# A two-block diffusion and sparse-attention kernel: column-halved opening modulation and a 112-candidate expert search

## The reference, cut to what matters

```python
m = (jax.nn.silu(c) @ w_mod[l] + b_mod[l]).reshape(B, N_MOD, D_MODEL)
mc = (jax.nn.silu(c_ctx) @ w_mod[l] + b_mod[l]).reshape(1, N_MOD, D_MODEL)
x = ffn_sublayer(x, m, 0, norm_g[l, 0], ffn_w_in[l, 0], ffn_w_out[l, 0])
# mod_norm(x, m, i, g) = rms_norm(x, g) * (1 + m[:, 3 * i + 1, None]) + m[:, 3 * i, None]
```

```python
v, i = lax.top_k(s, PEER_TOPK)
cand = (v[..., 0, :, None] + v[..., 1, None, :]).reshape(B, TB, PEER_HEADS, PEER_TOPK * PEER_TOPK)
tv, tj = lax.top_k(cand, PEER_TOPK)
w = jax.nn.softmax(tv, axis=-1)
a = jax.nn.gelu(jnp.einsum('btd,btpkd->btpk', hblk, u).astype(jnp.float32))
```

## Time and profile before

| | |
|---|---|
| median of three runs | 2854.39 us (2853.64 to 2857.55) |
| profiled execution, its own time | 2854.86 us |
| its span, first to last instruction | 2853.1 us |
| PE matmul busy | 2765.5 us (97%), 15702 records |
| DVE busy | 2095.5 us (73%) |
| ACT busy | 1211.4 us (42%) |
| POOL busy | 528.0 us (19%) |
| mean granted TensorE clock | 0.993 of full speed |

### The profile page before, as it was taken

The page is one execution under the profiler, slowest core; times in us unless marked ns, Lnnn a source line. Parts: engine busy times, 40 slices in busy tenths (PEclk is TensorE's granted clock), DMA queues, the critical chain, the costliest instruction groups (busy, mean ns, idle before and its releaser), DMA issues.

```text
span 2853.1 us, 40332 instructions
## 1 busy us (share of the span) xinstructions
PE 2765.5 (97%) x15702; PEld 2343.0 (82%) x15702; DVE 2095.5 (73%) x3770; ACT 1211.4 (42%) x2208; POOL 528.0 (19%) x447
## 2 busy tenths in 40 slices
PE   7999999989999999999988999998989999999998
PEld 4888887758888878888886999878989888888887
DVE  1989997477989897565766766755897677777776
ACT  2323234364222243222445545554556444444444
POOL 1111111500111111010040000344889100000000
PEclk9999999999999999999999999999999999999999
DMA  6455443223545445354441566423644555555564
GB/s 244 159 200 187 179 159 119 96 81 107 184 178 188 179 175 185 126 184 137 159 142 54 189 226 205 130 88 129 194 139 118 173 193 189 190 194 189 192 193 130
DMA packets 123262, 462.51 MB, mean 162 GB/s; under 512 B 13504, under 2 KB 26688, under 8 KB 109888
## 3 DMA queue, kind: packets, MB, share of 16 engines
q1 hardware_dynamic: 109248, 359.27, 38.1%
q0 software_dynamic: 13824, 100.67, 9.1%
HBM read 452.93 MB, written 6.95 MB: 161 GB/s over the span
## 4 chain that ended last, share of the span: by engine, by line
PE 85%; DVE 11%; issue 2%; ACT 1%; POOL 1%; DMA 0%; POOLq 0%; DVEq 0%; SPq 0%; ACTq 0%
PE bank L283 26%; PE bank L284 25%; PE bank L285 25%; DVE weight_lo L182 2%; PE bank L2309 2%; DVE extension_ffn L806 1%; PE bank L689 1%; PE bank L495 1%; DVE nmax L1280 1%; DVE arena L531 1%; PE bank L381 1%; PE bank L826 1%; PE bank L827 1%; ACT weight_hi L175 1%; DVE arena L2468 1%
## 5 line engine op out<-in xcount | busy, mean ns | idle before, releaser
L175 ACT ACTIVATE weight_hi<-weight_ring 128x512 fp32r<-128x512 f32 x1272 | 798.4, 630 | 1190.0 <-PE bank L285 1189.3
L182 DVE TENSOR_TENSOR weight_lo<-weight_ring,weight_hi 128x512 fp32r<-128x512 f32 x1110 | 839.2, 760 | 431.8 <-ACT weight_hi L175 429.9
L283 PE MATMUL bank<-operand_hi,weight_hi 128*128 128x256 f32 (+1 forms) x3168 | 1048.7, 331 | 26.3 <-DVE operand_lo L548 13.0
L284 PE MATMUL bank<-operand_lo,weight_hi 128*128 128x256 f32 (+1 forms) x3168 | 1034.6, 327 | 0.0
L285 PE MATMUL bank<-operand_hi,weight_lo 128*128 128x256 f32 (+1 forms) x3168 | 1034.1, 326 | 0.0
L283 PEld LDWEIGHTS bank<-operand_hi,weight_hi 128*128 128x128 f32 x3168 | 603.8, 191 | 96.9 <-issue 25.5
L284 PEld LDWEIGHTS bank<-operand_lo,weight_hi 128*128 128x128 f32 x3168 | 604.2, 191 | 53.7 <-issue 1.2
L285 PEld LDWEIGHTS bank<-operand_hi,weight_lo 128*128 128x128 f32 x3168 | 603.7, 191 | 50.6
L806 DVE SCALAR_TENSOR_TENSOR extension_ffn<-extension_ffn,silu_c 128x512 f32<-128x512 f32 x532 | 388.5, 779 | 1.7
L235 POOL TENSOR_TENSOR weight_lo<-weight_ring,weight_hi 128x512 fp32r<-128x512 f32 x162 | 214.6, 1334 | 431.2 <-ACT weight_hi L175 429.3
L283 PE MATMUL bank<-hidden_hi_ffn,weight_hi 128*128 128x512 f32 (+1 forms) x704 | 256.6, 364 | 4.0 <-DVE arena L1058 4.0
(11 more groups left out here) (259 smaller groups left out, 2616.5 us busy)
## 6 DMA issues: line engine op xcount, KB each, us to landing
weight_ring<-in_ffn SPq DMA_DIRECT2D x272, 512.0 KB, 3.5
weight_ring<-in_experts SPq DMA_DIRECT2D x256, 512.0 KB, 3.5
extension_ffn<-in_w_mods POOLq DMA_DIRECT2D x96, 1024.0 KB, 7.5
weight_ring<-in_w_mix SPq DMA_DIRECT2D x56, 512.0 KB, 3.5
weight_ring<-in_w_second SPq DMA_DIRECT2D x52, 512.0 KB, 3.6
spill<-early_retrieve SPq DMA_DIRECT2D x45, 128.0 KB, 3.8
arena<-spill SPq DMA_DIRECT2D x45, 128.0 KB, 3.4
extension_mixer<-in_rel_bias SPq DMA_DIRECT2D x2, 1536.0 KB, 6.8
```

Source lines behind the costliest of these rows:

```text
L175: nc.scalar.activation(self.hi[:, g % 2, h], self.ring[:, g % NS, h], ACT.Copy).then_inc(self.rounded, 1)
L182: self.nc.vector.tensor_tensor(self.lo[:, g % 2, h], self.ring[:, g % NS, h], self.hi[:, g % 2, h].bitcast(F32), ALU.subtract).then_inc(se ...
L283: nc.tensor.matmul(out, a_hi, b_hi, start=start and n == 0, stop=False)
L284: nc.tensor.matmul(out, a_hi, b_lo, start=False, stop=False)
```

## The change

In the opening, PE no longer sums eight pieces of squares: DVE adds them up (`gather`), and PE sums one piece, after modulation unit 4; the spread comes after unit 5. Each modulation unit goes in four pairs of matmuls, the first of a pair into partitions 0 and 1, the second into partitions 64 and 65 of a bank; four banks are used in turn, ACT copies both rows pairs, and the turn is now a matmul over 66 rows with a matrix `both` that adds the two halves. The turn comes two units behind. x is multiplied by the inverse root on DVE (`whiten`) before the gains are known; gain and shift are then applied by ACT in one instruction, and a second scaled copy (`again`), one token group by ACT and one by DVE, feeds the subtraction. The first weight unit is rounded and subtracted before the gains, and the second half of the second unit inside the operand loop. SP issues two weight units when modulation unit 6 is there and two when unit 7 is.

In retrieval, only the sums that can be among the 16 best are formed: left ranks 0 to 3 with all 16 right ranks and left ranks 4 to 15 with right ranks 0 to 3, 112 per head, in two instructions for all heads at once. `decode` gets three instructions to turn a position of 112 back into one of 256, and its integer positions and the index table lie in PSUM bank 7 instead of SBUF. The exponential of the first 128 tokens moves from behind down unit 18 to behind unit 16.

```diff
...
+class FirstNorm(Norm):
...
+    def whiten(self, dve):
+        dve.wait_ge(self.rstd_there.sem, self.rstd_there.at(1))
+        for kt in range(KT):
+            self.chip.nc.vector.tensor_tensor(self.h[:, kt, :], self.x[:, kt, :], self.rstd(0, T2), ALU.mult)\
+                .then_inc(self.scaled.sem, len(self.groups))
+    def round(self, act):
+        nc, n = self.chip.nc, len(self.groups)
+        act.wait_ge(self.gains_there.sem, self.gains_there.at(1))
+        for kt in range(KT):
+            if kt >= 4:
+                act.wait_ge(self.split_in.sem, self.split_in.at(kt - 3))
+            lo, hi = self.groups[1]
+            nc.scalar.activation(self.again[:, kt % 4, lo:hi], self.h[:, kt, lo:hi], ACT.Copy, scale=self.gain(kt, 1))
+            if kt == 2:
+                self.units.round(act, 0, 1, [1])
+            for g, (lo, hi) in enumerate(self.groups):
+                nc.scalar.activation(self.hi[:, kt, lo:hi], self.h[:, kt, lo:hi], ACT.Identity, bias=self.shift(kt, g),
+                                     scale=self.gain(kt, g)).then_inc(self.h_ready.sem, 1)
+    def again_scaled(self, dve, kt):
+        lo, hi = self.groups[0]
+        self.chip.nc.vector.tensor_scalar(self.again[:, kt % 4, lo:hi], self.h[:, kt, lo:hi], self.gain(kt, 0), None, ALU.mult)\
+            .then_inc(self.scaled_again.sem, 1)
+    def operands(self, dve):
+        self.again_scaled(dve, 0)
+        for kt in range(KT):
+            if kt + 1 < KT:
+                if kt >= 3:
+                    dve.wait_ge(self.split_in.sem, self.split_in.at(kt - 2))
+                self.again_scaled(dve, kt + 1)
+            dve.wait_ge(self.scaled_again.sem, self.scaled_again.at(kt + 1))
+            for g, (lo, hi) in enumerate(self.groups):
+                dve.wait_ge(self.h_ready.sem, self.h_ready.at(n * kt + g + 1))
+                last = nc.vector.scalar_tensor_tensor(self.lo[:, kt, lo:hi], self.again[:, kt % 4, lo:hi], self.shift(kt, g),
+                                                      self.hi[:, kt, lo:hi].bitcast(F32), ALU.add, ALU.subtract)
+            last.then_inc(self.split_in.sem, 1)
+            if kt == 1:
+                self.units.subtract(dve, 0, 1, [1])
+        dve.wait_ge(self.split_in.sem, self.split_in.at(KT))
...
-        sp.wait_ge(chip.mod_first[0].sem, 32)
-        self.stream.load(sp, 0, NS)
+        sp.wait_ge(chip.mod_first[2].sem, 32)
+        self.stream.load(sp, 0, 2)
+        sp.wait_ge(chip.mod_first[3].sem, 32)
+        self.stream.load(sp, 2, NS)
...
     def tensor(self, pe):
         chip, nc = self.chip, self.chip.nc
         def turn(l):
-            pe.wait_ge(self.copied.sem, self.copied.at(l + 1))
+            pe.wait_ge(self.copied.sem, self.copied.at(2 * l + 2))
             for b in range(2):
...
+                last = nc.tensor.matmul(chip.bank[2][:, 4 * l + 2 * b:4 * l + 2 * b + 2],
+                                        self.sums[0:66, l % 2, b * P:(b + 1) * P], chip.both[0:66, :], start=True, stop=True)
             last.then_inc(self.turned.sem, 1)
-        pe.wait_ge(chip.constants.sem, 1)
-        self.norm.sums(pe)
+        pe.wait_ge(chip.constants.sem, 2)
         pe.wait_ge(self.silued.sem, self.silued.at(1))
         for l in range(self.n):
             pe.wait_ge(chip.mod_first[l % self.slots].sem, 16 * (l // self.slots + 1))
+            if l >= 4:
+                pe.wait_ge(self.copied.sem, self.copied.at(2 * (l - 4) + 2))
+            for kt in range(0, KT, 2):
+                for j in range(2):
+                    last = nc.tensor.matmul(self.bank(l)[64 * j:64 * j + 2, 0:256], chip.silu_c[:, kt + j, :],
+                                            self.w[l % self.slots][:, (kt + j) * 256:(kt + j + 1) * 256],
+                                            start=(kt == 0), stop=(kt == KT - 2))
+            last.then_inc(self.first_summed.sem, 1)
             if l >= 2:
-                pe.wait_ge(self.copied.sem, self.copied.at(l - 1))
...
-            if l:
-                turn(l - 1)
-            if l == 1:
+                turn(l - 2)
+            if l == 4:
+                self.norm.sums(pe)
+            if l == 5:
                 self.norm.spread(pe)
+        turn(self.n - 2)
         turn(self.n - 1)
     def scalar(self, act):
         chip, nc = self.chip, self.chip.nc
+        def copy(l):
+            act.wait_ge(self.first_summed.sem, self.first_summed.at(l + 1))
+            if l >= 2:
+                act.wait_ge(self.turned.sem, self.turned.at(l - 1))
+            for j in range(2):
+                q = slice(64 * j, 64 * j + 2)
+                nc.scalar.activation(self.sums[q, l % 2, :], self.bank(l)[q, 0:256], ACT.Copy).then_inc(self.copied.sem, 1)
...
+        act.wait_ge(chip.constants.sem, 2)
         for kt in range(KT):
             self.norm.square(act, kt)
-        self.norm.root(act)
         for l in range(self.n):
...
-        for j in range(2):
-            self.units.round(act, 0, j)
+            if l == self.n - 1:
+                self.units.round(act, 0, 0)
+            copy(l)
+            if l == 3:
+                self.norm.root(act)
+        self.units.round(act, 0, 1, [0])
     def vector(self, dve):
         chip, nc = self.chip, self.chip.nc
+        def finish():
+            dve.wait_ge(self.turned.sem, self.turned.at(self.n))
...
         dve.wait_ge(self.loaded_x.sem, self.loaded_x.at(16))
+        for kt in range(1, KT):
+            self.norm.gather(dve, kt)
         self.norm.invert(dve)
...
-        finish_mod(chip, dve, 0, 0, 2)
-        for j in range(2):
-            self.units.subtract(dve, 0, j)
+        self.norm.whiten(dve)
+        self.units.subtract(dve, 0, 0)
+        finish()
+        self.units.subtract(dve, 0, 1, [0])
...
+CAND_ROWS = [(0, 0, 4, TOPK), (4 * TOPK, 4, TOPK, 4)]
+CANDS = 4 * TOPK + 4 * (TOPK - 4)
...
-TURN_AT, EXP_AT = [(ALONE - 1, 1), (ALONE + 14, 0)], [(ALONE - 2, 1), (ALONE + 13, 0)]
+TURN_AT, EXP_AT = [(ALONE - 1, 1), (ALONE + 14, 0)], [(ALONE - 4, 1), (ALONE + 13, 0)]
...
-        ixf = chip.part(E_IF, 2, 16, TOPK)
+        ixf = chip.bank[7][:, P:P + 16 * TOPK].rearrange("p (n k) -> p n k", k=TOPK)
...
-        jj, jf = chip.part(E_J, 2, SLOTS).bitcast(U32), chip.part(E_JF, 2, SLOTS)
+        jj, jf = chip.bank[7][:, P + 16 * TOPK:P + 16 * TOPK + SLOTS].bitcast(U32), chip.part(E_JF, SLOTS)
...
-        cand = chip.part(E_CAND, 2, PH, TOPK * TOPK)
+        cand = chip.part(E_CAND, 2, PH, CANDS)
...
             if first == 0:
-                step(nc.vector.tensor_copy(ixf[:, tt, :, :], ix[:, tt, :, :]))
+                if tt == 0:
+                    dve.wait_ge(self.table.sem, self.table.at(18))
+                step(nc.vector.tensor_copy(ixf, ix[:, tt, :, :]))
             vp = v[:, tt, :, :].rearrange("p (h two) k -> p h two k", two=2)
-            for h in range(first, last_h):
+            n = last_h - first
+            for at, a0, a1, nb in CAND_ROWS:
+                shape = [P, n, a1 - a0, nb]
                 last = nc.vector.tensor_tensor(
...
+                    cand[:, tt, first:last_h, at:at + (a1 - a0) * nb].rearrange("p h (a b) -> p h a b", b=nb),
+                    vp[:, first:last_h, 0, a0:a1].unsqueeze(3).to_broadcast(shape),
+                    vp[:, first:last_h, 1, 0:nb].unsqueeze(2).to_broadcast(shape), ALU.add)
...
+            step(nc.vector.tensor_scalar(jj, tj[:, tt, :], 4 * TOPK, 4 * TOPK, ALU.max, ALU.subtract))
+            step(nc.vector.tensor_scalar(jj, jj, 2, None, ALU.logical_shift_right))
+            step(nc.vector.scalar_tensor_tensor(tj[:, tt, :], jj, TOPK - 4, tj[:, tt, :], ALU.mult, ALU.add))
             for half in range(2):
-                step(nc.vector.tensor_scalar(jj[:, half, :], tj[:, tt, :], 4 if half == 0 else 15, None,
+                step(nc.vector.tensor_scalar(jj, tj[:, tt, :], 4 if half == 0 else 15, None,
                                              ALU.logical_shift_right if half == 0 else ALU.bitwise_and))
...
+                step(nc.vector.tensor_copy(jf, jj))
                 more(tt)
                 step(nc.vector.tensor_tensor(eq, iota16.unsqueeze(1).to_broadcast([P, SLOTS, TOPK]),
...
+                                             jf.unsqueeze(2).to_broadcast([P, SLOTS, TOPK]), ALU.is_equal))
                 more(tt)
                 e4 = eq.rearrange("p (h k) i -> p h k i", h=PH)
-                sub = ixf[:, tt, :, :].rearrange("p (h two) k -> p h two k", two=2)[:, :, half, :]
+                sub = ixf.rearrange("p (h two) k -> p h two k", two=2)[:, :, half, :]
...```

PE in the opening, from the program's first instruction to the first weight unit. Before (`arena` holds the squares, `extension_ffn` a modulation unit or the copied rows):

```order
L495 MATMUL bank<-ones,arena 128x2 x32
L689 MATMUL bank<-extension_ffn,silu_c 2x256 x16
L677 MATMUL bank<-ident,extension_ffn 128x2 x2
L517 MATMUL bank<-ident,rstd 128x128 x4
L689 MATMUL bank<-extension_ffn,silu_c 2x256 x8
```

71 lines of the change are left out of this document (40 added, 31 removed).

## The result

The changed kernel takes 2814.87 us (median of 4 runs, 2813.83 to 2818.67), the kernel before 2854.32 us in the same session (4 runs). The ratio is 0.9863, with a 95% interval of 0.9851 to 0.9875. The forecast was 2815, between 2808 and 2827. The profiled execution took 2814.13 us, 40.7 less than before, and its span is 2812.3. Of the runs of the kernel before that serve as comparison on other chips further down, one of 6799.85 us at a granted clock of 0.433 is left out.

A forecast was written before the change was run, and what follows sets the result against it. PE, busy nearly throughout, was taken as the bound, so gains come only from its waits or removable work. Opening 26.2 plus retrieval 13 gave 39.2 us off 2854.9: 2815.7, median 2815; forecast's range 2809 to 2822, 8-in-10 range 2808 to 2827.

The forecast's parts named there:

- eight pairs: Opening, PE: a modulation unit's matmuls run as side-by-side pairs, 1.75 us a unit at full rate, 3.5 at half.
- last turn: Opening, PE: the last modulation turn, waiting for ACT's copies and the rounding before the last copy, at 34.4 us.
- rival 1: Opening: halves do not overlap (first product near 50, 2827 us) or clock stays at half rate (2831); chance 0.12.
- the maximum: Retrieval, DVE: the row maximum is subtracted at 2063 us, at worst 2065, instead of 2079.8.
- batch 0: Retrieval, PE: the first batch starts at 2083.0 us, gain 5.8, with a new wait of 2.1 us.
- batch 24: Retrieval, PE: comes at 2138.8 us against 2152.29, 13.4 us gained, taken as 13 for possible half rate.
- PE's wait of 1.05 us before 2077.26: Retrieval, PE: unit 19 ends at 2079.1 without this wait, and the turn follows at once.
- The second decode's gain: Retrieval, DVE: casts with PSUM operands or results save 7 us there; three additions cost 0.8.
- A choose: Retrieval, DVE: 112 instead of 256 elements saves 1.65 us each, four of them 6.6.
- The landings at 2.43 us steps: Opening, transfers: modulation units 4 to 7 land at 21.8, 24.2, 26.6 and 29.1 us.
- Rival 2: Retrieval: ACT waits for DVE at the exponential, blocking rounding; 2829 to 2834 us; chance 0.20 together with another rival.
- the second multiply: Retrieval, DVE: by the rule it no longer holds POOL; by rows alone waits stay, second half gaining 2 us less.

The follow-up runs named there:

- unpacked: Changed kernel with all sixteen matmuls of a modulation unit going one after the other to partitions 0 and 1; 2827.73 us (0.9903).
- opening_only: Changed opening with the retrieval stage of the kernel before; 2826.87 us (0.9901).
- sbuf_numbers: Changed kernel with decode's integer steps, float indices and index table in SBUF instead of PSUM; 2822.57 us (0.989).
- exp_alone: Changed opening with the old retrieval, except that the first exponential stands behind gelu 16 instead of 18; 2831.89 us (0.9924).
- after_again: Changed kernel unaltered, run again on the same chip as later variants; 2819.02 us (0.9873).

## Why the prediction was right, step by step

**Opening.** First product 38.25 against 38.4. Steps: eight pairs 1.83 us from start to start of the next kind (31.59 to 33.42) against 1.75; turn 0.53 against 0.5; full rate from 16.5 against 15.5; whiten from 29.41 for 4.87 against 28.7 for 5.3; gains by 36.1 in both; last turn 34.95 against 34.4. The halves overlap (rival 1 was priced at 2827 with the first product near 50, and unpacked measured 2827.73 with it at 51.54). The Trainium skill, TensorEngine Tiling (Array Packing), section Key Properties, has a drain at a change of tiling mode. In after a turn starts 0.31 us after the start of the last pair, where pairs follow each other 0.215 apart, so 0.1 us at most is there to be a drain, and back from a turn to the pairs it is 0.18 against 0.11 within the turn. The same 0.31 stands in unpacked and in before, and the same 0.18 in unpacked, so the pairs added none. What the earlier rounding and whitening are worth by themselves no run shows. By places, from the start of the last turn to the first product it was 6.66 us (57.92 to 64.58) and is 3.30.

**Retrieval.** In the time of before (28.3 us added) the maximum was subtracted at 2062.6 against 2063, the exponential ran at 2072.7 as forecast, the turn at 2078.9 against 2079.1, batch 0 at 2082.8 against 2083.0 behind a wait of 1.98 against 2.1, and batch 24 at 2138.8 as forecast. That exactness is partly luck: in most profiles half rate behind that wait puts batch 24 1.6 us later. I had allowed 0.4 for it. That PE's wait of 1.05 us before 2077.26 would go, the working put down without a reason. It did: a wait of that size ahead of the turn stands in the four kernels with decode's numbers in SBUF (1.05 us in before, opening_only and, 7 us sooner, sbuf_numbers; 0.91 in exp_alone) and in none of the ten with them in PSUM. One reading of the working was off: PE ended unit 19 of the kernel before at 2080.36, 0.6 us after VectorE's subtraction of the maximum at 2079.76 and not before it; nothing in the sum hangs on it.

**The total.** The sum was 39.2 us; the profiled executions differ by 40.7, the medians by 39.5, and on another chip after_again saves 35.6. All lie in the range, but that forecast (2815) and median (2814.87) agree to 0.1 us is luck: the same kernel came out at 2819.02 there. The working priced the clock only at the places that the change touches; the 1.6 us of the second block are as much as the whole distance between the sum and the profile.

**Terms that were mis-sized.** The second decode's gain: 7 us less 0.8 forecast; it went from 30.3 us (2118.51 to the end of its last row at 2148.82) to 25.9 (2078.56 to 2104.49), 4.4. It cost nothing, since PE was not near the lead's end. A choose saved 1.5, not 1.65. The landings at 2.43 us steps were the term furthest off: modulation units 4 to 7 landed at 22.6, 25.4, 27.9 and 31.3, not at 21.8, 24.2, 26.6 and 29.1. PE came to unit 4 at 22.62, just as it landed (in eight of the other kernels with this order it waited 0.60 to 1.35 us for it, 1.15 in after_again), and to unit 7 at 31.59, 0.3 us after. Why unit 7 was late is open: two weight units were issued at 27.9 and 28.3 beside it, but in exp_alone, with the same beside it, it landed 2.4 us after unit 6 and not 3.5.

**A price that stays open.** Rival 2 priced a blocked exponential at PE's wait for weights, "7.1 less 2.4". The profile of exp_alone shows that wait in the place of the one before the turn, at no cost; the medians give 5.0, or 3.4 by chip. What the profile does show is that the price was worked out without the wait that already stood behind it (PE cannot pass the turn at 2084.40 either way), and such a price needs both.

**The port.** That numbers in PSUM would take the casts out of GpSimd's way was taken from the rows and supported by a rule; it is now shown by sbuf_numbers. The Trainium skill, SBUF — State Buffer, section SBUF: two separate sides, speaks of an exclusive lock for two-port modes and two SBUF inputs. The trace agrees in kind: 0.68 or 2.88 us for the same two additions, by whether GpSimd was at work. The prediction also said that the second multiply would then no longer hold GpSimd, where the rows alone would have kept the waits; the weighing of 3.01 us is 1.04 beside that multiply now, and 3.02 to 3.10 again in sbuf_numbers. The section on the change says too much of the five instructions behind the mapping: the reduction (L2618) still goes from SBUF to SBUF. It reads one operand and takes 2.29 us, 2.27 in the second decode of both kernels.

## What to carry to other kernels

Price a vector operation between SBUF operands twice, with GpSimd at work and without, and say which holds at its place: the factor was four here, and it decided two of my experiments. Before you sum gains of several means, ask whether they feed the same lead; either half of the retrieval change would have brought about two thirds of it or more. A program's start is worth a separate look: ordering work by arrival and packing 2-column products brought 26 of 40 us in a kernel whose PE was 97% busy. To compare variants under the spread of a whole run, measure from a place in the program to the next one, and count PE's time at 1.2 GHz in between.
